# Two transformer blocks on one core: the gap between the weight rings and the operand tiles becomes 256 bytes instead of 960

## The reference, cut to what matters

```python
for i in range(DEPTH):                        # first block, DEPTH = 2
    u = rmsnorm(h, norm_g[i]) @ w_in[i]       # (256, 2048) @ (2048, 5632)
    ya = conformer_conv(...) * silu(a_z)      # 31 taps, 1024 channels
    yb = window_attention(...) * silu(b_z)
    h = h + concatenate([ya, yb]) @ w_out[i]  # (256, 2048) @ (2048, 2048)
    e = rmsnorm(p[i] @ w_pe[i], pe_g[i])      # (256, 256) @ (256, 2048)
    h = h + e * sigmoid(h @ w_pg[i])
x = x + (fox_attention(q, k, v, log_f) * silu(gate)) @ fox_w_out      # q, k, v, gate from rmsnorm(x) @ fox_w_in
x = x + (swa_attention(q, k, v, sinks) * silu(gate)) @ swa_w_out      # q, k, v, gate from rmsnorm(x) @ swa_w_in
return rmsnorm(x, final_g)
```

## Time and profile before

| | us |
|---|---|
| median of 3 runs | 1827.05 (1826.09 to 1828.23) |
| the profiled execution, its own time | 1829.33 |
| its span, first to last instruction | 1827.5 |
| TensorE busy (matmul / weight load) | 1784.8 / 1703.9 |
| VectorE busy | 1313.7 |
| ScalarE busy | 900.0 |
| mean granted TensorE clock | 0.996 |

### The profile page before, as it was taken

How to read it: one execution, slowest core, us unless ns; L and a number is a source line. 1 busy time by engine, 2 the same in 40 slices (tenths; PEclk the granted TensorE clock), 3 DMA queues, 4 the chain that set the end, 5 groups by cost and what they waited for, 6 DMA issues and landing times.

```text
span 1827.5 us, 36452 instructions
## 1 busy us (share of the span) xinstructions
PE 1784.8 (98%) x14753; PEld 1703.9 (93%) x14753; DVE 1313.7 (72%) x2097; ACT 900.0 (49%) x1308; POOL 43.1 (2%) x48
## 2 busy tenths in 40 slices
PE   8999999999999999999999999999999999999997
PEld 7998999999999899999999799998989999899997
DVE  6998889886779987988776655555565656665764
ACT  5333565545533355455564363545454444466542
POOL 0000000000000000000000110100100000000000
PEclk9999999999999999999999999999999999999999
DMA  7566545555657664555555656666654565545452
GB/s 226 185 208 179 185 139 173 168 197 194 199 175 218 179 192 133 161 185 185 185 191 174 197 175 197 181 195 183 186 162 159 186 196 166 164 144 154 149 174 104
DMA packets 199109, 324.54 MB, mean 178 GB/s; under 512 B 14703, under 2 KB 66111, under 8 KB 198717
## 3 DMA queue, kind: packets, MB, share of 16 engines
q1 hardware_dynamic: 196653, 320.32, 56.6%
q10 hardware_dynamic: 2320, 2.31, 0.5%
HBM read 319.38 MB, written 2.69 MB: 176 GB/s over the span
## 4 chain that ended last, share of the span: by engine, by line
PE 75%; DVE 17%; ACT 4%; issue 1%; DMA 1%; SPq 0%; POOL 0%; ACTq 0%; DVEq 0%; POOLq 0%
PE g L480 62%; DVE w_lo L876 7%; DVE cacc L1111 6%; PE g L489 5%; PE att L565 2%; PE att L588 2%; PE att L608 2%; ACT w_hi L1450 2%; ACT u L1459 1%; DMA stage<-in_w_in_dram 1%; DMA stage<-in_fox_w_in_dram 0%; DVE u L1001 0%; PE att L759 0%; ACT L1459 0%; DVE q L897 0%
## 5 line engine op out<-in xcount | busy, mean ns | idle before, releaser
L876 DVE TENSOR_TENSOR w_lo<-stage,w_hi 128x1024 fp32r<-128x1024 f32 x577 | 703.9, 1226 | 428.9 <-ACT w_hi L1450 427.9
L1450 ACT CAST w_hi<-stage 128x1024 fp32r<-128x1024 f32 x577 | 598.1, 1048 | 652.5 <-PE g L480 485.0
L480 PE MATMUL g<-a_hi,w_hi 128*128 128x256 f32 x2496 | 705.5, 283 | 2.2 <-DVE w_lo L876 2.1
L480 PE MATMUL g<-a_hi,w_lo 128*128 128x256 f32 x2496 | 694.4, 278 | 0.0
L480 PE MATMUL g<-a_lo,w_hi 128*128 128x256 f32 x2496 | 694.3, 278 | 0.0
L480 PEld LDWEIGHTS g<-a_hi,w_hi 128*128 128x128 f32 x2496 | 471.4, 189 | 15.5 <-issue 11.5
L480 PE MATMUL g<-b_hi,w_hi 128*128 128x256 f32 x1696 | 476.6, 281 | 2.3 <-DVE w_lo L876 2.2
L480 PE MATMUL g<-b_hi,w_lo 128*128 128x256 f32 x1696 | 472.9, 279 | 0.0
L480 PE MATMUL g<-b_lo,w_hi 128*128 128x256 f32 x1696 | 472.8, 279 | 0.0
L480 PEld LDWEIGHTS g<-a_hi,w_lo 128*128 128x128 f32 x2496 | 469.3, 188 | 1.5 <-issue 1.2
L480 PEld LDWEIGHTS g<-a_lo,w_hi 128*128 128x128 f32 x2496 | 470.6, 189 | 0.0
(11 more groups left out here) (205 smaller groups left out, 1186.7 us busy)
## 6 DMA issues: line engine op xcount, KB each, us to landing
stage<-in_fox_w_in_dram SPq DMA_DIRECT2D x128, 512.0 KB, 3.9
stage<-in_w_in_dram SPq DMA_DIRECT2D x112, 512.0 KB, 3.8
stage<-in_swa_w_in_dram SPq DMA_DIRECT2D x72, 512.0 KB, 3.8
stage<-in_w_in_dram SPq DMA_DIRECT2D x128, 256.0 KB, 3.2
stage<-in_w_out_dram SPq DMA_DIRECT2D x64, 512.0 KB, 4.0
stage<-in_w_pg_dram SPq DMA_DIRECT2D x64, 512.0 KB, 4.1
stage<-in_fox_w_out_dram SPq DMA_DIRECT2D x32, 512.0 KB, 4.7
stage<-in_swa_w_out_dram SPq DMA_DIRECT2D x32, 512.0 KB, 4.5
```

What stands on the lines that cost most here:

```text
L480: mm = pe.matmul(acc[:, j * S:(j + 1) * S], w[:, slot, c0 + j * P:c0 + (j + 1) * P], xx[:, k, :], start=st and m == 0 and j % 2 == 0, stop ...
L876: dve.tensor_tensor(w_lo[:, slot, :], stage[:, slot, :], w_hi[:, slot, :].bitcast(F32), ALU.subtract).then_inc(*t.inc("w_split"))
L1450: act.copy(w_hi[:, slot, :], stage[:, slot, :]).then_inc(*t.inc("w_rounded"))
```

## The change

One constant changes. The unused tile between the rings and the operand tiles shrinks from 240 floats to 64 floats, from 960 to 256 bytes. No instruction is added, removed or moved on any engine: all five instruction lists are the same row for row. What changes is the start address of every tile behind `w_lo`.

```diff
-APART = 240
+APART = 64
```

## The result

The changed kernel takes 1867.41 us (median of 4 runs, 1866.49 to 1867.86) against 1827.64 us for the kernel before in the same comparison (median of 4 runs, 1826.09 to 1829.79). The ratio is 1.0212, with a 95% interval of [1.0196, 1.0229]. That is 40 us slower where 30 were forecast; it lies in both stated ranges. The profiled execution took 1866.49 us and its span is 1864.6 us, 37.1 us more than before.

What follows compares the result with a forecast made beforehand. TensorE, busy 98%, was taken as the bound through its pace in L480. Terms 28 + 1 + 1 = +30 us on the median 1827.05 gave 1857 us (+1.6%); likeliest case 1845 to 1870, wider range 1812 to 1886.

Steps and rivals of the forecast that it cites:

- Rival 1: All tiles: place doesn't matter and the pace step at `pe_hi` has another cause; time stays 1827 us; chance 0.14.
- I take the `pe` pace for all: L480 on the chain: every matmul at the side input's 118.7 ns; 18.0, 3.2 and 6.9, sum 28 us.
- the 1 us of the convolution: L480 beside VectorE: TensorE falls behind where it is fast, but its pauses swallow most of it; taken as 1 us.
- L489, taken as +1: L489, where activations are stationary: its pace has two levels, 233 and 229 ns; +1 us, between 0 and 2.
- Rival 4: L480: a collision in each matmul, 120 to 123 ns, worse than at `pe`; 1870 to 1899 us; chance 0.15.
- the picture of one passing in 512 bytes with the middle the worst place: L480: moving stream passes the weights' stream once per 512 bytes; at 256 mid-load, unavoidable, so 118.7 ns was taken.
- Rival 3: L480: 256 bytes, the middle, is the free place; all lock at 113.4 ns, 23 us less, 1804 us; chance 0.12.
- the likeliest case's own range: Whole kernel: 1845 to 1870 us around 1857, given as from the slow level everywhere to ten more.
- slow-level bound: L480 on the chain: all matmuls at the slow level, 3,400 x 4.5 + 2,300 x 2.2 = 20 us.
- the two `pe` runs should be at or above 118: Side input's matmuls with `pe_hi`/`pe_lo`, then 192 bytes past a multiple of 512: expected at or above 118 ns.
- the two levels are thrown at pauses and then held: L480: a fast (113.4 ns) or slow (about 118) level is entered after a TensorE pause and held for hundreds of matmuls.
- The bound from below: L759's quarter-length weight load still takes 113.8 ns; so 113.3 is the collision-free pace, and no gap goes below it.

Runs made afterwards that it cites:

- gap 0: Changed kernel with the unused tile left out, so the operand tiles begin on a multiple of 512 bytes; 1867.1 us.
- gap 192: Changed kernel with the unused tile at 192 bytes instead of 256; 1824.18 us at first, then 1832.26 us over 12 runs, ratio 1.0009 to the kernel before.
- the `w_lo` run: Changed kernel with 64 unused bytes between `w_hi` and `w_lo` and 192 behind `w_lo`, so only `w_lo` moved; 1852.52 us.

## Why the prediction was right or wrong

**Right: what bounds the kernel.** TensorE's pace is the time. No other engine's work changed, and VectorE's groups stayed at their mean.

**Right: that distance sets the pace and that the fast level goes.** Moving all tiles together does nothing; moving the rings alone brings the fast level back. Rival 1, in which place doesn't matter, is refuted: 113.4 against 120.0 ns for the same instructions. The rule of the Trainium skill (SBUF — State Buffer, "Who interferes with whom") that TensorE's two reads are independent and that it waits on no one doesn't hold in these runs, as far as the pace goes.

**Mis-sized: "I take the `pe` pace for all".** The term put all of L480 at 118.7 ns; it measured 120.0. On the prediction's own counts that is 9,700 x 1.3 = 13 us more, which makes 41 on the chain, and 42 with the 1 us of the convolution. Against this stand what the side input gave back, 192 x 5.4 = 1 us, and L489, taken as +1, which gave back about 384 x (231 - 227.5) = 1 us. 42 - 2 = 40, against 37.1 in the spans and 39.8 in the medians.

The two profiles can also be laid side by side matmul by matmul, as both have the same 14,753 in the same order. L480 on the main tiles then costs 42.7 us more, pauses included; L489 gives back 1.3 and the side input 3.7. Of these 3.7 only 1 is its pace. The rest is shorter pauses before two of its four groups of 48, 0.6 us each, and a dip of the clock in the profile of before: from 776 to 786 us the granted clock is 0.83, where the side input's last group runs. Another dip to 0.83 lies from 1030 to 1040 us; the changed kernel's profile has a mean of 0.999 against 0.996. By an estimate from these clocks (at most 0.17 x 10 us for each dip) they lengthened the profile of before by 1 to 3 us, so that 37.1 is too small by as much, and the 39.8 of the medians is the better measure. The throws of the kernel before move it too: gap 0, which is the same place, took 1867.1 us beside 1832.42, a loss of 34.7. Rival 4, a collision at each matmul at 120 to 123 ns, was in truth the better description, at its lower end.

**Wrong: the picture of one passing in 512 bytes with the middle the worst place.** The pattern repeats after 256 bytes, so 256 is no middle; it is the same place as 0. 384 was worse than 448 because it is 128 modulo 256 and not 192. The forecast's sign came from the nearest slow row more than from this picture, and that this row pointed the right way was luck: the places 128 and 0 modulo 256 both happen to be slow. Rival 3, the free middle, drew on the same picture and was wrong for the same reason.

**Too wide: the likeliest case's own range.** The slow-level bound of 20 us on 1827 gives 1847, and ten more than 1857 is 1867; the text has 1845 to 1870. The result is at the upper end of either.

**Wrong: "the two `pe` runs should be at or above 118".** They came to 113.3 ns, as the table modulo 256 says for 192.

**Right in part: the two levels are thrown at pauses and then held.** The two profiles of gap 192 show it for the long pieces. L489 with 256 columns changes level without a pause, so it isn't the whole rule.

**The bound from below** held: no long piece in any of the kernels is under 113.3 ns. The argument for it was weaker than it looked. The profile gives a load of 32 columns (L759) 108 ns and one of 128 columns 188 ns, so the short load isn't seen to be a quarter of the long one, nor absent.

**What stays open.** The sizes fit one quantity: 120.0 - 113.3 = 6.7 ns, two thirds of it is the slow level (117.8), four fifths give 118.7. That reads as a fixed loss on each colliding pair, with one in three or one in five escaping. It is argued from the numbers alone; the `w_lo` run fits it by its mean and not by its single distances. Why a stream at distance 192 locks into the one or the other level, and how the hardware holds these bytes, isn't shown either. That the two reads collide is the reading that is left, not something that a trace shows directly.

## What to carry to other kernels

Where TensorE is the bound, read its pace (length over count of a chain piece) and not the time of one matmul. If the same code has several paces at the same clock, try shifting the moving tiles against the stationary ones: here steps of 64 bytes over 256 bytes cover it, and an unused tile of 48 floats is the whole cost. Judge such a gap by the paces of several profiles or by a dozen runs, since a single time of a kernel with two levels can be off by 0.5%.

## What the runs showed of the hardware

TensorE's pace depends on the distance modulo 256 bytes between the moving tile and the stationary tiles loaded beside it. A matmul with 256 moving columns of split float32 takes 113.3 ns at best and 120.0 at distance 0. That holds with the roles turned as well: L489 with 256 columns of moving weights takes 120 ns at distance 0, and 114 or 118 in the kernel before. With 512 moving columns (L489) distance 0 is the best place instead, 227.5 ns against 229 and 233; why the length matters was not tested. And a moving tile 32 bytes off a multiple of 64 took 117 instead of 113.8 ns even beside a short weight load (L759).
